# A hybrid attention and pooling decoder step: the projection hands its queries over already turned, the passages between the stages are opened, and the first pool sums and the tail are reordered

## The reference, cut to what matters

```python
h = rmsnorm(x, g_pre)                       # x: tokens x 1024
z = h @ w_in                                # columns: q_lat 256, kv_lat 128, k_r 64, gates, pool input
q = rmsnorm(q_lat, g_q) @ w_uq              # 8 heads x (128 plain + 64 rotary)
q_r = rope(q[..., 128:], pos)
q_abs = einsum('bshn,rhn->bshr', q_nope, w_uk)
ckv_new, kr_new = rmsnorm(kv_lat, g_kv), rope(k_r, pos)
s = (q_abs . ckv + q_r . kr) * SCALE        # causal; decode also sees its paged cache
o = softmax(s) . ckv
y_att = (o @ w_uv * silu(z_att)) @ w_o_att
y_pool = (pool_mixer(u_pool) * silu(z_pool)) @ w_o_pool   # windows 2, 4, 8, 16
x = x + (sigmoid(g_att) * y_att + sigmoid(g_pool) * y_pool) @ w_out
y = rmsnorm(x, g_final)
```

## Time and profile before

| | us |
|---|---|
| median of 3 runs | 2245.72 (2243.98 to 2246.01) |
| the profiled execution | 2237.88, span 2236.1 |
| `project`, to the last copy of its queries | 0 to 234.3 |
| `attend` | 235.7 to 915.5 |
| `decode` | 920.6 to 987.9 |
| `merge` | 988.6 to 2236.1 |

### The profile page before, as it was taken

How to read it: one execution, slowest core, us unless ns; L and a number is a source line. 1 busy time by engine, 2 the same in 40 slices (tenths; PEclk the granted TensorE clock), 3 DMA queues, 4 the chain that set the end, 5 groups by cost and what they waited for, 6 DMA issues and landing times.

```text
span 2236.1 us, 32507 instructions
## 1 busy us (share of the span) xinstructions
PE 2145.5 (96%) x11994; PEld 1981.1 (89%) x11994; DVE 1295.6 (58%) x2646; ACT 1012.0 (45%) x1797; POOL 355.0 (16%) x496
## 2 busy tenths in 40 slices
PE   7999789999999999789999999999999999999997
PEld 6888668888888888579999999999999999999997
DVE  5565568788787778346544464446444554446434
ACT  5555545556555555344333443344333433344233
POOL 2333411110011010105000410023000500032000
PEclk9999899999999999899999999999999999999999
DMA  6454421111101020443544345344534344334532
GB/s 213 156 159 146 128 72 52 43 43 30 29 29 29 15 81 38 148 142 124 173 131 143 112 131 179 104 152 135 174 115 142 120 152 152 131 109 127 176 121 69
DMA packets 131001, 252.80 MB, mean 113 GB/s; under 512 B 17898, under 2 KB 80882, under 8 KB 129702
## 3 DMA queue, kind: packets, MB, share of 16 engines
q1 hardware_dynamic: 109214, 221.05, 30.4%
q10 hardware_dynamic: 19344, 17.30, 2.8%
q0 software_dynamic: 2304, 12.58, 1.5%
HBM read 208.34 MB, written 42.79 MB: 112 GB/s over the span
## 4 chain that ended last, share of the span: by engine, by line
PE 53%; POOL 1%; DVE 1%; DMA 0%; issue 0%; ACT 0%; POOLq 0%; SPq 0%; DVEq 0%; ACTq 0%
PE d_ps L121 52%; PE d_ps L1831 1%; POOL d_win L1674 1%; DMA d_wuv_f<-in_w_uv 0%; DVE d_y L1733 0%; POOL d_fstat L1655 0%; DVE d_y L1751 0%; POOL d_ols L83 0%; POOL d_fstat L1652 0%; ACT d_zs L1632 0%; DVE d_y L1735 0%; DVE d_gat L83 0%; POOL d_win L1679 0%; DVE d_y L1816 0%; DVE d_wr L83 0%
## 5 line engine op out<-in xcount | busy, mean ns | idle before, releaser
L121 PE MATMUL d_ps<-d_ht,d_wr 128*128 128x412 f32 x3840 | 735.8, 350 | 2.4 <-PEq L1069 1.7
L121 PEld LDWEIGHTS d_ps<-d_ht,d_wr 128*128 128x128 f32 x3840 | 716.9, 188 | 6.4 <-issue 2.7
L83 DVE TENSOR_TENSOR d_wr<-d_ws,d_wr 128x1024 fp32r<-128x1024 f32 x260 | 321.2, 1236 | 560.5 <-ACT d_wr L1008 560.5
L1008 ACT ACTIVATE d_wr<-d_ws 128x1024 fp32r<-128x1024 f32 x260 | 275.4, 1059 | 607.3 <-PE d_ps L121 595.9
L917 PE MATMUL b_ps<-kt,k_qs 128*128 128x512 f32 (+3 forms) x1600 | 346.0, 374 | 12.4 <-POOL k_qs L83 8.8
L917 PEld LDWEIGHTS b_ps<-kt,k_qs 128*128 128x128 f32 x1600 | 281.5, 193 | 65.8 <-POOL k_qs L83 12.2
L936 PE MATMUL b_ps<-b_pt,kv 128*128 128x512 f32 x816 | 230.3, 413 | 3.0 <-DVE b_pt L83 3.0
L818 ACT ACTIVATE b_p<-b_p,b_bias 128x1024 f32<-128x1024 f32 (+7 forms) x192 | 171.7, 896 | 103.5 <-DVE b_low L879 98.9
L83 DVE TENSOR_TENSOR b_pt<-b_ps,b_pt 128x512 fp32r<-128x512 f32 x272 | 182.0, 688 | 61.1 <-ACT b_pt L825 59.9
L825 ACT ACTIVATE b_pt<-b_ps 128x512 fp32r<-128x512 f32 x272 | 156.9, 597 | 121.4 <-PE b_ps L936 66.8
L121 PE MATMUL d_ps<-d_mrg,d_wr 128*128 128x412 f32 x960 | 189.9, 353 | 0.0
(11 more groups left out here) (194 smaller groups left out, 2129.9 us busy)
## 6 DMA issues: line engine op xcount, KB each, us to landing
d_ws<-in_w SPq DMA_DIRECT2D x260, 512.0 KB, 3.5
out_q<-a_qout SPq DMA_DIRECT2D x17, 768.0 KB, 3.3
a_x<-in_x ACTq DMA_DIRECT2D x17, 512.0 KB, 3.8
out_ht<-a_hf SPq DMA_DIRECT2D x17, 512.0 KB, 4.2
d_hf<-out_ht SPq DMA_DIRECT2D x20, 412.0 KB, 3.5
d_olf<-out_olat SPq DMA_DIRECT2D x40, 206.0 KB, 3.0
k_qf<-out_q SPq DMA_DIRECT2D x32, 256.0 KB, 2.7
k_qf<-out_q SPq DMA_DIRECT2D x128, 64.0 KB, 2.6
```

What stands on the lines that cost most here:

```text
L83: return e.tensor_tensor(low, source, high.bitcast(f32), ALU.subtract)
L121: mm = pe.matmul(out, stationary(a, k), moving(b, k), start=first and k == 0 and a + b == 0, stop=last and k == depth - 1 and a == 1)
L1008: act.activation(ahead["wr"][k % 2][:, 0, :, :], ahead["ws"][k % 4][:, :, :], ACT.Copy).then_inc(ahead["w_hi"], 1)
```

## The change

In `project`:

- The host also gives `x` turned (`x_t`, one more 512 KB load per tile). DVE multiplies it with the gain and the inverse root in 8 instructions of 128x128; the inverse root comes spread over the partitions by one PE transpose of a broadcast column into `ps_r`. The 8 transposes of `h` and ACT's two copies to `hf` go.
- The query product has its operands exchanged: `wq` is stationary, `qt` moving, for groups of tiles (`GROUPS_Q`: 8 + 128 + 128 tokens, then pairs of 256). 12 blocks of 6 products give queries that are already turned. The 12 transposes and the copies to `qabs` go. ACT copies blocks from a ring of 4 PSUM banks to `qout`; DVE rotates from them with angle tables in turned form (`turn`).
- The decode tile comes first, 8 columns wide. A group's blocks are multiplied in two steps, 3 and 4 steps after its last tile. The loop is written out, not a loop with registers.
- `load_q` reads the new layout of `q`.

At the passages: `attend` and `decode` share their PSUM tensors, the wait for `o_out` goes from the end of `attend` to `decode` (before `turned_exponents`) and `merge` (before the first `load_latent`), and PE turns the first cached rows of two sequences (`TURNED_AHEAD`) at the end of `attend`. In `merge`, four constants are issued from ACT's queue, POOL's first sum no longer waits for them, and the tail gives squares to DVE, does the products with `g_final` before the root is there and splits the scaling between ACT and DVE by rows.

The diff, cut to its core:

```diff
+GROUPS_Q = ((0, 1, 2),) + tuple((n, n + 1) for n in range(3, NT, 2))
+RING = 4
+def query_parts():
+    parts, at = [], 0
+    for k in range(len(GROUPS_Q)):
+        per_bank = 512 // NQ[k]
+        for half in range(2):
+            order = [tuple(range(a, a + per_bank)) for a in range(0, HG, per_bank)]
+            order.insert(len(order) // 2 if per_bank == 1 else 0, None)
+            for heads in order:
+                count = 2 if heads is None else len(heads)
...
@@ project, every engine
+        def halves(i):
+            return [(k, a) for k, members in enumerate(GROUPS_Q) for a in range(2) if members[-1] + 3 + a == i]
@@ project, sync
+                    sp.wait_ge(h_ok, i + 1)
+                    at = TILES[i] * P
+                    sp.dma_start(io["ht"][:, :, at:at + P], hf[:, :, :]).then_inc(h_out, 16)
+                    if i + 2 < NT:
+                        load_xt(i + 2)
@@ project, vector
+            def tokens(n):
+                dve.wait_ge(spread_ok, n + 1)
+                dve.wait_ge(xt_in[n % 2], 16 * (n // 2 + 1))
+                wait(dve, h_out, 16 * n)
+                wait(dve, ht_ok, n)
+                for k in range(KD):
+                    h = dve.scalar_tensor_tensor(out=hf[:, k, :], in0=xt[:, n % 2, k, :], scalar=gpre[:, k:k + 1],
+                                                 in1=ps_r[:, 0:P], op0=ALU.mult, op1=ALU.mult)
+                h.then_inc(h_ok, 1)
+                dve.wait_ge(h_ok, n + 1)
+                wait(dve, lat_ok, n)
+                dve.tensor_copy(ht[:, 0, :, :], hf[:, :, :]).then_inc(ht_hi, 1)
+                dve.wait_ge(ht_hi, n + 1)
+                split(dve, ht[:, 1, :, :], hf[:, :, :], ht[:, 0, :, :]).then_inc(ht_ok, 1)
@@ project, tensor
+            def spread(n):
+                pe.wait_ge(x_rinv_ok, n + 1)
+                wait(pe, h_ok, n)
+                pe.transpose(ps_r[:, 0:P], x_rinv[n % 2].to_broadcast([P, P]), ident[:, :]).then_inc(spread_ok, 1)
+            for i in range(1, LAST_STEP + 1):
+                if 2 <= i < NT:
+                    spread(i)
+                if i <= NT:
+                    n = i - 1
+                    pe.wait_ge(ht_ok, n + 1)
...
+                for k, a in halves(i):
+                    pe.wait_ge(nt_lo, GROUPS_Q[k][-1] + 1)
+                    for part in in_half[k, a]:
+                        for other in part.freed_by:
+                            pe.wait_ge(qcos_ok if other.heads is None else qout_a, other.count)
+                        for columns, bank, at in part.blocks:
+                            mm = three_products(pe, ps_q[bank][:, at:at + NQ[k]],
+                                                lambda b, c: wq[:, b, c, columns:columns + P],
+                                                lambda b, c: qt[:, k % 2, b, c, 0:NQ[k]], KQ)
+                        mm.then_inc(q_ok, 1)
@@ attend, sync
-            for n in range(2):
-                sp.wait_ge(o_out[n], 16 * units // 2)
@@ attend, tensor
+            pe.wait_ge(s_sb, sum(kind == "S" for kind, *_ in orders["PE"]))
+            for j in range(TURNED_AHEAD):
+                pe.wait_ge(early["cache_in"][j], 32)
+                turn_keys(pe, ident, early["cn"][j], early["rn"][j], 0, ps_t[j], ps_s[j],
+                          early["turned_c"], early["turned_r"])
@@ merge, sync and scalar
-            sp.dma_start(pscale[:, :], io["pool_scale"]).then_inc(const_in, 16)
-            sp.dma_start(head[:, :, :], io["head"]).then_inc(const_in, 16)
-            sp.dma_start(hist[:, :, :], io["hist_t"]).then_inc(const_in, 16)
-            sp.dma_start(gfin[:, :], io["g_final"].partition_broadcast(P)).then_inc(const_in, 16)
+            act.dma_start(head[:, :, :], io["head"]).then_inc(const_in, 16)
+            act.dma_start(hist[:, :, :], io["hist_t"]).then_inc(const_in, 16)
+            act.dma_start(pscale[:, :], io["pool_scale"]).then_inc(const_in, 16)
+            act.dma_start(gfin[:, :], io["g_final"].partition_broadcast(P)).then_inc(const_in, 16)
@@ merge, gpsimd
-            pool.wait_ge(const_in, CONSTS)
-                    after(pool, (u_sb, c * NG + g + 1), (small_ok, 3), *([(pl_f, c * NG + g - 1)] if g > 1 else []))
+                    after(pool, (u_sb, c * NG + g + 1), (small_ok, 1), *([(pl_f, c * NG + g - 1)] if g > 1 else []))
+                    if c == 0 and g == 0:
+                        pool.wait_ge(const_in, CONSTS)
                     if g == 0:
-                        after(pool, (pick_in, c * 16 + 16))
+                        after(pool, (pick_in, c * 16 + 16), (small_ok, 3))
@@ merge, the tail: scalar
-            for s, rows in enumerate(BLOCKS):
+            for s in range(2):
-            for s in range(2):
-                act.activation(y[:, s, 0:WIDE], y[:, s, 0:WIDE], ACT.Copy, scale=last[:, 3, s:s + 1]).then_inc(last_a, 1)
+            for s in (0, 3):
+                rows = BLOCKS[s]
+                act.activation(y[0:rows, s, :], y[0:rows, s, :], ACT.Copy, scale=last[0:rows, 3, s:s + 1]).then_inc(last_a, 1)
@@ merge, the tail: vector
+            for s in (2, 3):
+                dve.tensor_tensor_reduce(out=gated[0:rows, 0:D - WIDE], in0=y[0:rows, s, WIDE:D], in1=y[0:rows, s, WIDE:D],
...
+            for s in (2, 3, 0, 1):
...
+                dve.tensor_tensor(y[0:rows, s, WIDE:D], y[0:rows, s, WIDE:D], gfin[0:rows, WIDE:D],
...
             dve.wait_ge(last_stat, 3)
+            for s in (1, 2):
+                dve.tensor_scalar(y[:, s, :], y[:, s, :], last[:, 3, s:s + 1], None, ALU.mult).then_inc(last_d, 1)
```

More of the change, by code:

```diff
@@ new lines, in project, with stores @@
+        kv_hi = sem("kv_hi")
+        parts = query_parts()
+        in_half = {(k, a): [part for part in parts if (part.k, part.half) == (k, a)]
+                   for k in range(len(GROUPS_Q)) for a in range(2)}
+        rotated = {key: [part for part in some if part.heads is None][0] for key, some in in_half.items()}
+        copied = {key: [part for part in some if part.heads is not None] for key, some in in_half.items()}
+        def stores(k):
+            return 16 * sum(len(members) for members in GROUPS_Q[:k])
@@ L296, in step @@
+                    own(pool.tensor_tensor(ksin[:, :], lat[:, K0:K0 + ROPE], sin[:, tile, :], ALU.mult))
                     wait(pool, nt_ok, n)
@@ L366, in step @@
+            square(0)
+            for part in range(2):
+                act.wait_ge(wlat_in[part], 16)
+                act.activation(wlat[:, 0, 4 * part:4 * part + 4, :], wlat_f[:, 4 * part:4 * part + 4, :],
+                               ACT.Copy).then_inc(wq_hi, 1)
+                square(1 + part)
+            for i in range(1, LAST_STEP + 1):
+                if i <= NT:
                     n = i - 1
-                    wait(act, lat_ok, n + 1)
+                    act.wait_ge(lat_ok, n + 1)
@@ L391, in _ @@
-            steps(act, step, columns, prepare, ahead=ahead)
+                if i == LAST_STEP - 1:
+                    for u in range(2):
+                        query_high(act, keep, u)
+                for k, a in halves(i):
+                    wait(act, q_out[a], stores(k))
+                    for part in copied[k, a]:
+                        act.wait_ge(q_ok, part.number + 1)
+                        bank, heads, width = part.banks[0], part.heads, NQ[k]
+                        act.activation(qout[:, a, heads[0]:heads[-1] + 1, 0:width],
+                                       ps_q[bank][:, 0:len(heads) * width].rearrange("p (h t) -> p h t", h=len(heads)),
+                                       ACT.Copy).then_inc(qout_a, 1)
@@ L543, in _ @@
-            steps(pe, step, prepare=prepare)
+                if i == 1:
+                    pe.wait_ge(wq_in, 48)
+                    for k in range(KQ):
+                        for a in range(2):
+                            for hh in range(4):
+                                head = 4 * a + hh
+                                mm = pe.matmul(ps_q[2 * a + k][:, hh * R:hh * R + R], wuq_t[:, head, k * P:k * P + P],
+                                               wuk_t[:, head, :], start=True, stop=True)
+                            mm.then_inc(absorbed, 1)
@@ L1076, in decode @@
         ident, kt = keep["ident"], keep["kt"]
-        bank = [ctx.enter_context(nc.psum_tensor(f"c_ps{n}", [P, 512], f32)) for n in range(8)]
+        whole = early["ps"]
+        bank = [whole[n] for n in (6, 7, NS, NS + 1, NS + 2, 0, 1, 2)]
         ps_s, ps_c, ps_r, ps_new = bank[0:2], bank[2:5], bank[5:7], bank[7]
@@ L1166, in _ @@
                     weights_high(act, ahead, 0, AHEAD_W.index(n))
+            for n in range(2):
+                act.wait_ge(o_out[n], 16 * PT * NGRP // 2)
             turned_exponents(0)
@@ L1233, in _ @@
             maximum(1)
+            for n in range(2):
+                dve.wait_ge(o_out[n], 16 * PT * NGRP // 2)
             turned_exponents(0)
@@ L1932, in build @@
         early["rn3_at"] = nc.sbuf_base + (NDEC - EARLY_N) * RUN * R * 4
```

(10 more changed lines are left out.)

603 lines of the change are left out of this document (297 added, 306 removed).

## The result

The changed kernel takes 2204.9 us (median of 4 runs, 2204.1 to 2206.6) where the kernel before takes 2245.5 beside it: a ratio of 0.983, 95% interval 0.981 to 0.984. The prediction was 2208.2. The profiled execution has a span of 2202.6 against 2236.1, 33.5 less; foreseen were 37.5 less.

A forecast was written before the change was run, and what follows sets the result against it. PE, busy 96% of the span, was taken as the bound. Project -31.6, passage -4.4, start of merge +0.6 and tail -2.1 sum to -37.5 us: 2200.4 profiled, median 2208.2; range 2199 to 2226.

The forecast's parts named there:

- Tile on PE: In project: 20 transposes and a wait of 0.33 go, so a tile takes 10.1 us on PE, 2.15 less.
- The ring: In project: PE never waits for one of 4 banks, each copied in about 0.7 us while another fills for 1.5.
- the rival of late transfers: In project: the store of hf lands late, DVE waits and PE behind it; 1.2 us per tile, 2224; chance 0.11.
- DVE: In project: DVE does not take over as bound, with 8.4 of 10.1 us per tile; eight new instructions take 2.74.
- this rival: In project: DVE becomes the bound, deciding only from 1.7 us more; 11 us per tile, 2220; chance 0.16.
- Start of project: First six tiles are slower: second tile at 31.2 us, step 5 to 66.0, step 6 to 76.1.
- the 76 that the prediction named as a sign of being wrong: In project: a start longer than 76 us for the first six tiles would show the prediction wrong.
- Attend and the passage: Attend unchanged (0, bounds 0 to +3); passage to decode -4.4 us without SP's wait for the olat stores; turning ahead brings nothing.
- the 680 that the prediction named as a sign: Attend taking longer than the 680 us from 235.7 to 915.5 would show the prediction wrong.
- Decode: The block after attend: moves earlier with its start, its own length unchanged, 0 us.
- Start of merge: POOL's first sum moves ahead, but constants on ACT's queue cost up to 1.9 us: +0.6, bounds -1.3 and +2.
- Tail: End of merge: squares shared with DVE (0.8 to 1.1) and faster scaling (0.4 to 1.2): -2.1 us, bounds -1.2 and -2.6.

The follow-up runs named there:

- dve_extra8: Changed kernel with eight more 128 x 128 products on DVE per tile of project, from the sixth tile on, into an unread buffer: 2204.6 us.
- before_split: Kernel before with each of its 18 query products of 512 columns per tile done as two of 256: 2236.9 against 2237.5 us, ratio 1.0006.
- pe_extra8: Changed kernel with eight more transposes of the identity on PE per tile in steps 5 to 17 of project, into an unread bank: 2211.3 us.
- old_tail: Changed kernel with the tail of the kernel before (four squares on ACT, root products in two pieces per block, stores in order): 2206.3 us.

## Why the prediction was right

**Tile on PE: right, 0.4 us too long.** 9.71 against 10.1; 24 latent products take 4.97 from start to start (5.02 taken), norm transposes 0.36 (0.45), the spread 0.03 (0.12), and 36 query products 4.35 (4.5). The bound that I chose for the last, 0.125 each, was above the 0.121 that came. From the sixth step's latent products to the last it is 107.8 against 111.6, 3.9 more gain than foreseen. The ring, for which the prediction had "no wait", costs 0.65 in each of the two steps with 264 columns and nothing later. What the profile moves, 243 GB/s, is the 240 expected, and in the steady state DVE waits for PE alone: the rival of late transfers has no place there.

**DVE: right in kind.** 7.7 of 9.7 us, against 8.4 of 10.1; each of the eight new instructions shows 0.34 but starts 0.27 behind the last, so they take 2.2 and not the 2.74 of the sum (which has 2.4 for them at the start). dve_extra8 shows that 1.8 us more per tile are free; the prediction let this rival decide from 1.7.

**Start of project: 2.6 us too short.** The latent products of the sixth step stand at 68.6, not at 66.0: the store of `hf` landed near 29.5 and not near 26.7, and the first two sets took 7.8 and 7.4 where the later ones take 5.2. The edit that takes the store out of the way brings 4.4; the turned identity brings up to 2.0. The first six steps end at 79.4, beyond the 76 that the prediction named as a sign of being wrong: its account of the start did fail, and the shorter tiles made up for it. With their 3.9 it makes -33.0 instead of -31.6.

**Attend and the passage: right.** -4.5 foreseen as -4.4; undoing it costs 4.3 there, and turning ahead brings nothing. POOL's first fetch comes 36.4 earlier, foreseen as 36. What I had not priced is the 0.55 to 0.7 by which the fetch lands later. `attend`, from its first scores to its last instruction, is 680.9 long: over the 680 that the prediction named as a sign, but within what it varies by between profiles.

**Decode: the step that failed.** The sum took it as moved and not changed, though the change puts PE's wait for the rotary keys ahead of the four latent transposes (lines of the change that the diff's core does not show). A term of +2.3 us was put at nothing. The wait cost 1.2 of it, which the edit shows. The rest is argued, not shown: PE idles 4.4 us at the fourth sequence instead of 1.5, and its first scores still run at half clock behind that (0.53 at 897 to 902.6): their 16 products with the rotary keys take 1.64 where the kernel before took 1.04, and the step 5.39 against 4.62.

**Start of merge: the delay was right, its price was not.** `w_uv` came 1.75 later through the constants on ACT's queue (12.62 against 10.87 behind `merge`'s first product; 1.3 against the profile of the kernel before), within the 1.9 of the prediction, and ate what moving POOL's first sum had gained: POOL reached the product behind `hsum` 16.55 behind `merge`'s first product, as in the kernel before (16.53). The wait for `ols` grew from 3.39 to 4.17, just over the 4 named. Up to the end of that wait the stage is 0.4 longer, near the +0.6; the products behind it, at a granted clock of 0.60, add 1.5, a price that the prediction has not. But in before_split the old `merge` waits 4.43 and runs as slowly, so +1.7 against the kernel before is one pair of profiles and no steady cost of the change. What stands is the comparison of medians on one chip: about 4 us less with the constants on SP's queue.

**Tail: half of it.** -1.1 to -1.4 against -2.1. The squares brought their 1.1; the faster products brought 0 to 0.3 of the 1.0, as the four stores leave SP one after another. The prediction had counted the last store as sooner.

**The sum.** The profiled span fell by 33.5, where 37.5 were foreseen, and the medians by 40.6. The prediction of 2208 was right to 3 us because these two errors are opposite, and that is luck. The profiled execution of before (2237.9) lies 7.8 below its median, and the prediction added those 7.8 to the kernel after, whose profiled execution lies 0.3 below its own. The mechanism holds better than that: PE's work per tile, the passage and the absence of the rivals came as told. The kernel before also takes 2237.5 on one of the chips, but its first profile shows the gaps of the small products that this chip does not. No run of it near 2245 has a profile, so where those 8 us lie is not settled; on the chip of 2237.5 the gain would be nearer to the 33.5 of the spans (dve_extra8, whose `project` ends 0.4 later than the changed kernel's, took 2204.6 there, ratio 0.986).

## What to carry over

Ask of each engine not only how busy it is but add dummy work to one at a time: eight idle transposes and eight idle products told in two runs who bounds the tile and by how much. When a wait is moved past other work of the same engine, count what it now stands in front of, even where the diff looks like a mere regrouping. A few microseconds of PE's waiting can have two prices, the wait and the slower products behind it. And look at the same stretch in every profile at hand, those of the kernel before too, before calling a difference there the work of an edit: the wait for `ols` came out at 0.8 to 4.4 us.

## Not expected of the hardware

- The same 64 products of 8 columns took 1.0 us without a gap on one chip (pe_extra8) and about 6 us, with four to seven gaps of 0.2 to 1.8 us that nothing but issue ended, on the others. The DMA share was 0.99 to 1.03 in that stretch (890 to 902.6 in the changed kernel), and still 0.90 where there was no gap (900 to 902 in pe_extra8); the cause was not tried.
- Behind a wait of 3.39 us for `ols` PE went on at full clock in the kernel before and in old_tail (24 products in 4.5 from start to start), but in dve_extra8 at a granted clock of 0.59 (5.4). Behind the waits of 4.17 and 4.43 in nine profiles it was 0.50 to 0.61 each time (5.9 to 6.6).
- DVE busy 98% of the time beside a PE that is busy 100% cost PE nothing.
